# The expert loop of TensorE: two branches per pair, or one branch over the whole pair

## The reference, cut to what matters

```python
def hierarchical_moe(hin, w_group, b_group, w_router, b_router, w_gate, w_up, w_down):
    xt = hin.reshape(b * s, d)
    g_prob = softmax(xt @ w_group + b_group)            # 4 groups, the best one is taken
    g_w, g_idx = lax.top_k(g_prob, 1)
    e_logits = ... xt @ w_router + b_router, of the chosen group
    e_val, e_idx = lax.top_k(e_logits, 2)               # 2 of its 4 experts
    gates = one_hot(g_idx * 4 + e_idx) * (g_w * softmax(e_val))
    for e in range(16):
        hid = silu(xt @ w_gate[e]) * (xt @ w_up[e])     # 1024 -> 512
        y = y + gates[:, e:e + 1] * (hid @ w_down[e])   # 512 -> 1024
    return y
```

## Time and profile before

| | us |
|---|---|
| median of 3 runs | 1206.73 |
| all runs | 1206.06, 1206.73, 1208.35 |
| the profiled execution: its own time | 1208.35 |
| its span | 1206.7 |
| PE busy in it | 1145.2 (95%) |
| DVE busy | 379.0 (31%) |
| ACT busy | 283.6 (24%) |
| mean of what the DMA engines moved | 292 GB/s |

### The profile page before, as it was taken

One profiled execution on the slowest core, in us unless ns is written; L12 is line 12 of the kernel. 1 busy time (PEld: TensorE's weight loads), 2 busy tenths in 40 slices (PEclk: granted clock), 3 DMA queues, 4 the chain that ended last, 5 costly groups with the idle time before them and its releaser, 6 DMA issues.

```text
span 1206.7 us, 17047 instructions
## 1 busy us (share of the span) xinstructions
PE 1145.2 (95%) x6930; PEld 671.8 (56%) x6931; DVE 379.0 (31%) x1025; ACT 283.6 (24%) x598; POOL 83.7 (7%) x141
## 2 busy tenths in 40 slices
PE   3999998999999999999899999998999999999997
PEld 0755544344444367664344444443886888867883
DVE  0344334121211137652521221112541334342213
ACT  2224421011111121054311111112101454552201
POOL 0200011000000000140000000000001133200000
PEclk8899998999999999999999999999999999999999
DMA  9998877999999987796679999999695453344000
GB/s 362 358 328 344 281 278 281 425 413 424 429 429 429 415 329 273 269 241 238 285 320 415 424 430 428 429 429 397 230 269 181 144 162 119 130 153 146 9 16 35
DMA packets 68867, 352.77 MB, mean 292 GB/s; under 512 B 5284, under 2 KB 7500, under 8 KB 49356
## 3 DMA queue, kind: packets, MB, share of 16 engines
q1 hardware_dynamic: 61656, 340.68, 72.8%
q0 software_dynamic: 5488, 8.12, 2.7%
q10 hardware_dynamic: 1668, 3.21, 0.7%
HBM read 350.84 MB, written 1.15 MB: 292 GB/s over the span
## 4 chain that ended last, share of the span: by engine, by line
PE 81%; DMA 13%; DVE 3%; ACT 1%; issue 1%; ACTq 0%; SPq 0%; DVEq 0%
PE bank L493 28%; PE bank L831 21%; PE bank L531 11%; DMA ring<-in_moe_w_up 11%; PE bank L801 3%; PE bank L852 3%; PE bank L546 2%; DMA arena<-in_ev_w_s 2%; PE bank L1124 1%; PE bank L517 1%; PE bank L505 1%; PE bank L739 1%; PE bank L682 1%; PE bank L706 1%; PE bank L605 1%
## 5 line engine op out<-in xcount | busy, mean ns | idle before, releaser
L493 PE MATMUL bank<-arena,ring 128*128 128x256 f32 x1536 | 341.9, 383 | 2.8 <-ACT arena L1228 1.7
L831 PE MATMUL bank<-ring,arena 128*32 128x512 f32 x3072 | 335.1, 593 | 7.8 <-issue 3.5
L493 PEld LDWEIGHTS bank<-arena,ring 128*128 128x128 f32 x1536 | 293.0, 192 | 47.5 <-issue 7.8
L831 PEld LDWEIGHTS bank<-ring,arena 128*32 128x32 f32 x3072 | 101.3, 110 | 229.0 <-issue 227.5
L531 PE MATMUL bank<-ring,arena 128*128 128x512 f32 x320 | 139.8, 594 | 0.8 <-ACT arena L1367 0.8
L531 PEld LDWEIGHTS bank<-ring,arena 128*128 128x128 f32 x320 | 60.2, 190 | 73.2 <-issue 71.6
L2170 DVE TENSOR_TENSOR arena<-arena,bank 128x512 f32<-128x512 f32 x16 | 11.0, 688 | 195.5 <-PE bank L831 195.5
L801 PEld LDWEIGHTS bank<-arena 128*128 128x128 f32 x512 | 62.4, 203 | 14.2 <-issue 11.7
L801 PE MATMUL bank<-arena 128*128 128x128 f32 x512 | 65.4, 289 | 2.2 <-DVE arena L2138 2.2
L1669 DVE SCALAR_TENSOR_TENSOR arena<-arena,cv 128x256 f32<-128x256 f32 x144 | 58.5, 480 | 0.3
L1408 ACT ACTIVATE arena<-bank 128x512 f32<-128x512 f32 x16 | 9.6, 597 | 207.7 <-PE bank L831 207.7
(11 more groups left out here) (320 smaller groups left out, 913.2 us busy)
## 6 DMA issues: line engine op xcount, KB each, us to landing
ring<-in_moe_w_gate SPq DMA_DIRECT2D x32, 2048.0 KB, 14.3
ring<-in_moe_w_up SPq DMA_DIRECT2D x32, 2048.0 KB, 17.2
ring<-in_moe_w_down SPq DMA_DIRECT2D x32, 2048.0 KB, 13.5
ring<-in_w_ada SPq DMA_DIRECT2D x24, 2048.0 KB, 17.4
ring<-in_w_in SPq DMA_DIRECT2D x16, 2048.0 KB, 10.2
ring<-in_w_c SPq DMA_DIRECT2D x6, 2048.0 KB, 33.8
ring<-in_ev_w_in SPq DMA_DIRECT2D x5, 2048.0 KB, 14.5
ring<-in_od_w_in SPq DMA_DIRECT2D x5, 2048.0 KB, 15.6
```

What stands on the lines that cost most here:

```text
L493: mm = pe.matmul(ps[k0][:, t * S:(t + 1) * S], w[:, k, c:c + P], rhs[:, k, :], start=(k == 0), stop=(k == KT - 1))
L831: mm = pe.matmul(bank[col:col + CHUNK, :], lhs[:, k, col:col + CHUNK], ring[:, (s0 + e) % RING, cut], start=start, stop=stop, tile_positio ...
```

## The change

The two choices per pair become one. `by_split` is now called once per pair, with a function `pair(n)` that holds all of a pair's work, so each of the three cases has its own copy of gather, transposes and scatter too. `turn_weights` is merged into `down`, and the wait on `g_cur_ready` moves into it. The aligning instruction is gone. The hints are other ones: a hint in the middle of a pair, ahead of the scatter, names the target of the branch that ends the pair's code, in cases 2 and 1. One more stands behind the loop, and names the place behind `left_over_tokens`. For that the branch over this code is now two branches, the second of them with the hint. No arithmetic and no transfer changes.

```diff
-                def by_split(what, which, emit, ahead=None):
+                def by_split(which, emit):
 
-                    name = {n: f"{what}_{n}_of_{layer}" for n in ("rare", 1, 3, 2, "done")}
+                    name = {n: f"pair_{n}_of_{layer}" for n in ("rare", 1, 3, 2, "done")}
                     pe.br_cond(which == 2, name[2], name["rare"])
                     with nc.body(name[2], valid_engines=[pe.engine]):
-                        emit(2)
-                        leaves = pe.br(name["done"])
-                        if ahead is not None:
-                            leaves.branch_hint(ahead)
+                        leaves = emit(2)
+                        pe.br(name["done"]).branch_hint(leaves)
                     with nc.body(name["rare"], valid_engines=[pe.engine]):
                         pe.br_cond(which == 1, name[1], name[3])
                     with nc.body(name[1], valid_engines=[pe.engine]):
-                        emit(1)
-                        pe.br(name["done"])
+                        leaves = emit(1)
+                        pe.br(name["done"]).branch_hint(leaves)
...
-                pe.addr_align(256, 44, 0)
                 with pe.Fori(0, PAIRS) as j:
 
-                    which = pe.snap(split_reg)
-                    ahead = pe.mark_branch_hint_location()
-                    by_split("gate_up", which, lambda n: gate_up(j, n), ahead)
-                    with pe.If(j > 0):
-                        results(j - 1)
-                    with pe.If(j < PAIRS - 1):
-                        gather(j + 1)
-                    turn_hid(j)
-                    with pe.If(j > 0):
-                        scatter(j - 1)
-                    turn_weights(j)
-                    by_split("down", which, lambda n: down(j, n))
-                    pe.wait_ge(sem("g_cur_ready"), j + (done + 1))
+                    def pair(n):
+                        gate_up(j, n)
+                        with pe.If(j > 0):
+                            results(j - 1)
+                        with pe.If(j < PAIRS - 1):
+                            gather(j + 1)
+                        turn_hid(j)
+                        leaves = pe.mark_branch_hint_location()
+                        with pe.If(j > 0):
+                            scatter(j - 1)
+                        down(j, n)
+                        return leaves
+
+                    by_split(pe.snap(split_reg), pair)
                 group_columns(group)
+                to_next = pe.mark_branch_hint_location()
                 results(PAIRS - 1)
                 scatter(PAIRS - 1)
...
-            def state_turned(layer):
+            def state_turned(layer, ahead):
...
-                pe.br_cond(pe.snap(split_reg) > 0, f"late_pe{layer}", f"on_pe{layer}")
+                pe.br_cond(pe.snap(split_reg) > 0, f"late_pe{layer}", f"pass_pe{layer}")
+                with nc.body(f"pass_pe{layer}", valid_engines=[pe.engine]):
+                    pe.br(f"on_pe{layer}").branch_hint(ahead)
```

More of the change, by code:

```diff
@@ L871, in turn_hid, with down @@
                     mm.then_inc(sem("hidT_full"), 1)
-                def turn_weights(j):
+                def down(j, n):
                     pe.wait_ge(sem("pick_g_ready"), j + (done + 1))
@@ L885, in turn_weights @@
                         pe.wait_ge(sem("x_cur_dve"), j + (done + 2))
-                def down(j, n):
                     pe.wait_ge(sem("hidT_ready"), j + (done + 1))
@@ L898, in down @@
                             mm.then_inc(unit_done, 2)
+                    pe.wait_ge(sem("g_cur_ready"), j + (done + 1))
                 pe.reg_load(split_reg, split[0:1, layer, 0:1])
@@ L922, in experts @@
                 unit[0] = first + 6 * PAIRS
-            def state_turned(layer):
+                return to_next
+            def state_turned(layer, ahead):
                 r = 2 * layer + 2
@@ L1052, in _ @@
             turn_tile(1, 1)
-            experts(0)
-            state_turned(0)
+            state_turned(0, experts(0))
             by_channel("od0", hT, arrived=state_there(2))
@@ L1102, in _ @@
             turn_tile(3, 1)
-            experts(1)
-            state_turned(1)
+            state_turned(1, experts(1))
             by_channel("in0", hT, arrived=state_there(4))
```

## The result

The changed kernel takes 1214.92 us (median of 4 runs, 1213.45 to 1216.75) against 1206.85 us (4 runs, 1206.06 to 1208.35): ratio 1.0070, interval 1.0055 to 1.0086, so 8.1 us slower. I had forecast 1210.1, 3.4 slower, with a range up to 1213.0: the sign was right, the size wrong. The profiled execution of after has a span of 1216.5 us, 9.8 more than that of before.

What follows compares the result with a forecast made beforehand. PE (95% busy) bounds the early pairs, late weights from saturated DMA the later ones. Terms 0.2 (loop 0) - 0.2 (behind) + 3.7 (loop 1) - 0.3 (behind) = +3.4 us, forecast 1210.1; 8-in-10 range 1205.8 to 1213.0.

Steps and rivals of the forecast that it cites:

- Pages and the length of a fetch: TensorE's code: pages of 256 instructions, one fetched ahead, kept over the loop; 6.2 to 6.3 us from wanting to running one.
- Second choice removed: Pairs 1 to 7: a 0.19 us branch and a comparison go, both beside queued products; worth nothing.
- Down products of pair 0: Less issue ahead of the first pair's down products: 0.5 us off in layer 1, 0.2 in layer 0.
- Exit of pair 0, layer 0: Branch ending layer 0's first pair, now about four pages far: -0.2 to +1.2 us, taken as +0.2.
- Head of layer 1: Start of layer 1's loop: case 1's code two pages on, not asked for, so first product +4.2 us.
- Exit of that pair: Branch ending layer 1's first pair: hint about 8 us ahead, no other page to fetch, nothing late.
- Behind loop 0: Code after layer 0's loop: the hinted page holds 237 instructions from the landing place, so 0.23 us goes (-0.2).
- Behind loop 1: Code after layer 1's loop: some 36 instructions remain to the page boundary instead of 31; -0.3 us.
- The page at the head: Rival: the page at layer 1's head is there in time, 4.2 us falls away, 1205.9 us; chance 0.17.
- Code was not dropped: Rival: layer 1 touches eight pages, only seven held, so pair 1 waits again: +4, 1214 us; chance 0.10.
- Layer 0's exit: Rival: two fetches ahead of layer 0's first-pair exit instead of one, +3 us on PE, 1212 us; chance 0.08.

Runs made afterwards that it cites:

- place 200 alone: Changed kernel with the code behind each loop aligned to place 200 of its 256-instruction page, layer 1's head kept at 87: 1220.77 us, ratio 1.0113.
- aligned to 44: Changed kernel with the aligning instruction put back ahead of both expert loops (head 44 beyond a multiple of 256 instructions): 1215.83 us, ratio 1.0057.
- the kernel with place 20: Changed kernel with the code behind each loop aligned to place 20 of the next page, layer 1's head kept at 87: 1207.74 us, ratio 1.0001.
- early kernel: Changed kernel with the in-pair hint moved to the pair's first instruction, ahead of the gate products: 1209.37 us, ratio 1.0036.
- the one without pair hints: Changed kernel with only the hint behind the loops and none in the pairs: 1222.12 us, ratio 1.0132.
- copy 1 first: Changed kernel with the code of case 1, which layer 1's first pair takes, placed first in layer 1: 1209.88 us, ratio 1.0019.
- late: Changed kernel with the in-pair hint moved behind the first 8 down products: 1224.44 us (single run).
- place 200 (two kernels): Changed kernel with code behind each loop at place 200 of its page: alone 1220.77 us; with case 1 first in layer 1, its head at 136, 1217.36 us.
- early with copy 1 first: Changed kernel with the in-pair hint as the pair's first instruction and case 1 first in layer 1: 1210.17 us, ratio 1.0014.

## Why the prediction was wrong, step by step

*Pages and the length of a fetch:* right. Pages of 256 instructions, one fetched ahead, 6.2 us from wanting one to running it: 27 of the 31 long branches in after and the experiments lie between 5.6 and 6.5 us. The other four are 7.0 us (place 200 alone) and 7.2 us (aligned to 44), where two fetches ran at the same time, and the two of 4.4 and 4.7 us with the late-served hints of the kernel aligned to 44. That the later pairs of layer 0 run without a fetch held in every kernel.

*Second choice removed:* 0, right; from the second pair on no gap of PE is put down to a branch.

*Down products of pair 0:* -0.6 in layer 1 for -0.5, right. In layer 0 the 1.22 us of the earlier trace rows became 1.26, no gain of 0.2.

*Exit of pair 0, layer 0:* taken at +0.2 with -0.2 to +1.2; measured -1.4 for the whole loop, outside these bounds. A loop 0 that ends over 1 us earlier was one of my own signs of being wrong, and it ended 1.0 earlier by the clock of the whole run and 1.4 by its own start. The hint was served, the branch took 1308 ns, hidden under queued products, and the 1.71 us went. I had taken the DMA engines for saturated, so that this would come back as waits for weights. These only went from the 1.6 us in three of the earlier trace rows to 1.9 in four:

```profile
PE bank L829 <- DMA ring<-in_moe_w_up: 1.9, 4, 0.5
```

In after 232 to 436 us ran at a share of 1.01, and still the loop took 1.4 us less: the cap was there from the earlier trace rows but worth less than I put on it.

*Head of layer 1:* +4.2 forecast, +4.0 measured, the choice 6.2 us long as forecast; right. This was the step thought to decide.

*Exit of that pair:* forecast at nothing, measured +1.4. The branch took 2918 ns at 642.8 us and PE idled 1.18 us. The hint's page was fetched at 643.3, only after the branch had begun, since the page of the branch is entered shortly ahead of it. I had counted from the hint, not from that entry.

*Behind loop 0:* this is the step that failed. The prediction put -0.2 there because "in layer 0 the hinted page holds 237 instructions": it took for granted that the hint would have fetched the page. The page was not there, the branch took 6.0 us, and it cost 4.8 and 1.4 of clock, so +6.2. Taking the stall away by place (the kernel with place 20) gave back 7.2 us at the median (8.3 by the two ratios, 1.0070 and 1.0001). With -0.2 replaced by +6.2 and nothing else changed, the sum is 9.8, which is the difference of the two spans. That it meets it so well is luck: the other misses, listed below, about cancel.

*The clock:* in no term. Each of the two long idle times is followed by a stretch at 1.2 GHz that cost 1.4 us against before, which has one of half the length behind loop 0 and none at the head.

*Behind loop 1:* right in size (-0.3 forecast, -0.1 measured).

*The rivals:* all three fell. The page at the head was not in time: the first product was 4 us late. Code was not dropped: no pair waited for code again. Layer 0's exit did not turn worse: its branch took 1308 ns. The Trainium skill ("Runtime: NRT & Kernel Launch", "Instruction fetch mechanics") says that a branch out of the two-page window forces a fetch before execution goes on: the long branches agree for pages never visited; for pages visited before, the runs disagree, with no code fetch in 232 to 436 us of before nor of after.

*In sum:* the failed step makes 6.4 us; the clock at the head (+1.4) and the exit of layer 1's first pair (+1.4) about cancel against the gain in loop 0 (-1.6 beside the forecast) and the -1.3 in loop 1, where the waits for weights fell from 1.6 us to 0.7. I had spread the chances over the head, where the pages were counted, and given none to a hint behind the loop that isn't served. The medians differ by less than the profiles (8.1 against 9.8).

What stays open: when a hint given in the page that already runs is served. Served behind loop 0: in both profiles of the early kernel and in the one without pair hints. Not served: in after, with copy 1 first, late, with place 200 (two kernels), and in all three profiles of early with copy 1 first.

## What to carry to other kernels

Count code in pages of 256 instructions whenever a branch goes further than the next page: on the first visit to a page not yet asked for, TensorE's branch took 5.6 to 6.5 us here, some 4 to 5.5 us of it without products, and a slow clock followed. A hint helped where it stood ahead of the entry of its branch's page; given later, it was served in some kernels and not in others. What worked behind both loops in both kernels that had it was to place the code so that a branch enters the page ahead of the landing place 6 us or more before it is needed. At the loop's head it was to put the copy that the data take first where the code is entered.

## What the runs showed of the hardware that I had not expected

- A branch that lands on a page that is there already is followed by a fetch, 3.1 to 3.5 us after it ends (433.6 in the early kernel, 438.9 in before, where no hint stands). With place 20 the fetches at 423.9 and 428.3 us, 6.5 and 6.7 us ahead of the long jump, fit this, though the hint beside the entry isn't ruled out there.
- A hint for a branch in a page entered later is served at that entry: in the early kernel the fetch moved 26 us after the hint.
- A hint given in the page that already runs was served in some kernels, with the fetch 6.3 to 6.6 us behind it, and in others not at all, with the same instructions up to there.
- 4.35 and 5.46 us without products were followed by 3.4 and 6.8 us at 1.2 GHz; each cost 1.4 us more than the same place in before.
